# The delta rule's small steps placed by readiness, age and recent use of TensorE, between the dense blocks of a whole-model kernel

## Chip, cores, metric

The kernel runs on one core of a Trainium2 chip, in one launch. The metric is the device time of a run in microseconds; lower is better.

## What is computed

The input is 256 tokens of width 1024, in float32. Sixteen meta tokens are put before them (272 columns in the kernel). The first block has two layers, a gated DeltaNet and an mLSTM, each followed by a convolutional FFN; a second block of two layers has pooling, sparse attention and memory attention. The change matters in the gated DeltaNet. It is, cut to its core:

```
proj = h @ w_in                                   # dense: q, k, v, z, and the gates
kb = kc * bc[..., None]
a_mat = jnp.eye(CHUNK) + jnp.einsum('bhnid,bhnjd->bhnij', kb, kc) * decay * strict
sol = lax.linalg.triangular_solve(a_mat, rhs, left_side=True, lower=True)
attn = jnp.einsum('bhnid,bhnjd->bhnij', qc, kc) * decay
def step(S, xs):                                  # over the chunks, one after the other
    v_new = u_c - jnp.einsum('bhck,bhkv->bhcv', w_c, S)
    o_c = jnp.einsum('bhck,bhkv->bhcv', qd_c, S) + jnp.einsum('bhij,bhjv->bhiv', att_c, v_new)
    S = S * gt_c[..., None, None] + jnp.einsum('bhck,bhcv->bhkv', kt_c, v_new)
    return S, o_c
o = rms_norm(o, norm_w) * jax.nn.silu(z)
return o.reshape(B, L, GDN_VAL_DIM) @ w_out       # dense
```

The kernel takes chunks of 16, 128 and 128 tokens (c = 0, 1, 2) and inverts the triangular matrix itself, by doubling.

## The kernel before

**Dense work.** Weights stream from HBM through `ring` in slabs. Each half slab is split into a high part (`splitH`, by ScalarE) and a low part (`splitL`, by VectorE or GpSimd), and every dense product is three matmuls: aH with splitH, aH with splitL, aL with splitH. A dense block is these three for one slice of 128 of the contraction; in the DeltaNet stage they are 128x272. An output tile is eight blocks. The main program `gdn()` has four phases of eight tiles (`GDN_TILES`), one for each of four groups of heads (g = 0 to 3), and then 16 tiles for z. `gdn_out()` follows, the projection w_out, whose blocks read arenaR.

**Small steps.** Beside the main program run tasks, as generators, for group g and chunk c: `core(g)` makes keys, decays and products (its front), and then the recurrence over the chunks; `inv(g, 0)` and `tri(g, c)` invert the triangular matrices by levels of 16x16, 32x32 and 64x64 products; `vtr(g)` transposes v; `out(g, c)` normalizes and transposes the output. Each step is a handful of float32 matmuls that write one PSUM bank, and then work of VectorE, ScalarE or GpSimd before the task's next step can start. A float32 matmul that isn't a transpose has two records in the trace, so that `x4` in the order is `x8` there.

**The order.** `weave()` lays all into one list, `flow`, before the program is written, and each engine's instructions follow this list (`replay`). On the chip each engine runs its own in order and waits on semaphores. `weave()` runs a `Clock` for each engine, which holds planned costs; `settle()` moves them on. Each yield of a task gives the time at which it is due again: the end of the engines' planned work and 0.2 us. `one(due)` takes the task that has been due longest. It is called after each dense block until no task is due:

```
        if v != "go":
            while one(True):
                pass
```

A step is put off only where no PSUM bank of its pool is idle (`room`). Some steps hold the main program up: `until("vuse", 0, 2)` ahead of phase 3 (the recurrence of group 0 must have used its v), the z tiles wait for `until("out", gz, c)` of earlier groups, and `gdn_out()` waits at its ninth block for `until("out", 3, c)`, the last step of the last group. There is nothing dense to run at such a place.

## Time and profile before

| | |
|---|---|
| median of 3 runs | 1634.6 us (1634.51 to 1642.09) |
| the profiled execution, its own time | 1634.17 us |
| its span | 1632.4 us |
| PE busy | 1582.0 us of the span |
| mean granted TensorE clock | 0.952 of full speed |

The span is from the first to the last instruction; 1.8 us of the execution lie around it. PE is TensorE's matmul row. The granted clock is 1.00 at 2.4 GHz and 0.50 at 1.2 GHz; a mean between the two tells the share of time at each.

### The profile page before, as it was taken

The page shows a single profiled execution, that of the slowest core. Times are in us where ns is not written, and L with a number is a line of the kernel's source. Part 1 is how long each engine was busy: PE and PEld are TensorE (multiplying, and loading weights), DVE is VectorE, ACT ScalarE, POOL GpSimd, SP SyncE. Part 2 cuts the span into 40 slices and gives each one's busy share as a digit, 9 for nine tenths or more (in the row PEclk, how much of TensorE's full clock was granted, in tenths as well). Part 3 has the DMA queues.
Part 4 walks back from the last instruction along what each step waited for, and adds up shares of the span by engine and source line. Part 5 has one row for each costly group of instructions (what it writes and reads, how often), then busy time and mean ns, then how long its engine had stood idle before and what let it go on. Part 6 is the DMA issues. An engine that isn't in the chain of part 4 may idle for free.

```text
span 1632.4 us, 35024 instructions
## 1 busy us (share of the span) xinstructions
PE 1582.0 (97%) x14201; PEld 1488.6 (91%) x14201; DVE 1102.6 (68%) x2253; ACT 944.8 (58%) x1988; POOL 346.8 (21%) x412
## 2 busy tenths in 40 slices
PE   8998999999999999999999999999999989999998
PEld 6987987899899999987899999889999989899998
DVE  4776686558588864766689965667766666676663
ACT  6652664456376654546476754547676554667754
POOL 4231222133133322000423421003101210031010
PEclk9987797899799999999799999999999999999999
DMA  6320222035265554342346766545444645454452
GB/s 206 117 80 3 80 82 63 28 104 169 100 201 174 172 182 144 126 132 92 128 151 196 199 218 201 160 130 167 132 153 156 215 162 168 140 168 142 143 172 88
DMA packets 64976, 230.41 MB, mean 141 GB/s; under 512 B 7312, under 2 KB 9488, under 8 KB 64816
## 3 DMA queue, kind: packets, MB, share of 16 engines
q1 hardware_dynamic: 59792, 217.67, 42.3%
q0 software_dynamic: 4160, 8.98, 1.8%
q8 instruction: 113, 1.85, 0.5%
q10 hardware_dynamic: 864, 1.52, 0.3%
q14 instruction: 47, 0.39, 0.1%
HBM read 222.91 MB, written 5.24 MB: 140 GB/s over the span
## 4 chain that ended last, share of the span: by engine, by line
PE 77%; DVE 12%; ACT 5%; issue 3%; DMA 1%; POOL 1%; ACTq 0%; SPq 0%; DVEq 0%; POOLq 0%
PE ps L623 75%; DVE splitL L2305 4%; DVE arena L2313 3%; PE ps L627 3%; ACT splitH L1699 2%; ACT arena L1704 1%; DVE mixT L2310 1%; DVE arena L2310 1%; ACT L1704 1%; DVE arena L2321 1%; ACT sq L1704 1%; DMA ring<-wst 1%; POOL sq L3129 1%; ACT arenaR L1704 0%; DVE mixT L2313 0%
## 5 line engine op out<-in xcount | busy, mean ns | idle before, releaser
L2305 DVE TENSOR_TENSOR splitL<-ring,splitH 128x512 fp32r<-128x512 f32 x767 | 564.6, 765 | 244.0 <-ACT splitH L1699 235.5
L623 PE MATMUL ps<-aH,splitH 128*128 128x256 f32 (+2 forms) x2232 | 661.0, 297 | 13.4 <-DVE arena L2321 5.8
L623 PE MATMUL ps<-aH,splitL 128*128 128x256 f32 (+2 forms) x2232 | 640.5, 288 | 0.0
L623 PE MATMUL ps<-aL,splitH 128*128 128x256 f32 (+2 forms) x2232 | 626.8, 287 | 0.0
L1699 ACT ACTIVATE splitH<-ring 128x512 fp32r<-128x512 f32 x824 | 479.9, 622 | 130.5 <-PE ps L623 120.8
L623 PEld LDWEIGHTS ps<-aH,splitH 128*128 128x128 f32 x2232 | 429.8, 193 | 28.6 <-issue 11.5
L623 PEld LDWEIGHTS ps<-aH,splitL 128*128 128x128 f32 x2232 | 430.1, 193 | 0.0
L623 PEld LDWEIGHTS ps<-aL,splitH 128*128 128x128 f32 x2232 | 422.2, 192 | 0.4
L623 PE MATMUL ps<-arenaR,splitH 128*128 128x256 f32 (+2 forms) x1856 | 348.0, 288 | 3.0 <-POOL arenaR L3129 1.6
L623 PEld LDWEIGHTS ps<-arenaR,splitH 128*128 128x128 f32 x1856 | 290.9, 191 | 4.8 <-POOL arenaR L3129 1.9
L623 PE MATMUL ps<-arenaR,splitL 128*128 128x256 f32 (+2 forms) x928 | 264.2, 285 | 0.0
L1704 ACT ACTIVATE arena<-ps 128x256 f32<-128x256 f32 (+10 forms) x261 | 94.7, 367 | 185.5 <-PE ps L623 164.0
L623 PE MATMUL ps<-arena 32*32 32x32 f32 (+6 forms) x3144 | 177.6, 237 | 11.5 <-DVE arena L2310 9.6
L623 PEld LDWEIGHTS ps<-arenaR,splitL 128*128 128x128 f32 x928 | 176.7, 190 | 0.0
L623 PEld LDWEIGHTS ps<-arena 32*32 32x32 f32 (+4 forms) x3144 | 132.3, 137 | 45.8 <-issue 26.7
L2313 DVE SCALAR_TENSOR_TENSOR arena<-ps,vec_sb,arena 128x271 f32<-128x271 f32 (+4 forms) x275 | 135.2, 492 | 35.9 <-ACT arena L1704 30.4
L3129 POOL TENSOR_TENSOR arena<-arena 128x272 f32<-128x272 f32 (+4 forms) x79 | 73.2, 931 | 287.1 <-DVE arena L2313 145.2
L1704 ACT ACT_TABLE_LOAD x92 | 118.0, 1283 | 4.2 <-PEq L3589 1.7
L1704 ACT ACTIVATE arena<-ps,vec_sb 128x272 f32<-128x272 f32 (+5 forms) x154 | 74.2, 496 | 63.2 <-PE ps L623 61.7
L3124 POOL TENSOR_TENSOR splitL<-ring,splitH 128x512 fp32r<-128x512 f32 x57 | 77.4, 1367 | 141.5 <-ACT splitH L1699 140.7
L1704 ACT ACTIVATE arena<-arena 128x256 f32<-128x256 f32 (+10 forms) x137 | 64.2, 480 | 49.3 <-DVE arena L2313 26.8
L2321 DVE COPY arena<-ps 128x256 f32<-128x256 f32 (+9 forms) x138 | 51.8, 382 | 40.3 <-PE ps L623 34.6
(212 smaller groups left out, 1282.5 us busy)
## 6 DMA issues: line engine op xcount, KB each, us to landing
ring<-wst SPq DMA_DIRECT2D x412, 512.0 KB, 3.9
mem_scratch<-arenaR POOLq DMA_DIRECT2D x16, 128.0 KB, 4.3
arenaR<-mem_scratch POOLq DMA_DIRECT2D x4, 512.0 KB, 8.2
rel_scratch<-arena POOLq DMA_DIRECT2D x8, 255.5 KB, 3.6
arena<-x SPq DMA_DIRECT2D x2, 512.0 KB, 4.9
arena<-mem POOLq DMA_DIRECT2D x2, 512.0 KB, 4.3
arena<-rel_scratch POOLq DMA_DIRECT2D x1, 1024.0 KB, 9.1
out<-arena ACTq DMA_DIRECT2D x4, 256.0 KB, 2.1
```

The source lines that it names most:

```text
L623: return pe.matmul(out, lhsT, rhs, start=start, stop=stop)
L627: return pe.transpose(out, in_, ident[0:n, 0:n])
L1699: act.activation(hi, raw, ACT.Copy, bias=0.0, scale=1.0).then_inc(*inc(("hi", q)))
L1704: return act.activation(out, in_, f, bias=bias, scale=scale, accum_out=accum)
L2305: dve.tensor_tensor(lo, raw, hi.bitcast(F32), ALU.subtract).then_inc(*inc(("lo_dve", q)))
L2310: return dve.tensor_tensor(out, x, y, op)
L2313: return dve.scalar_tensor_tensor(out=out, in0=x, scalar=s, in1=y, op0=op0, op1=op1)
L2321: return dve.tensor_copy(out, x)
L3124: pool.tensor_tensor(lo, raw, hi.bitcast(F32), ALU.subtract).then_inc(*inc(("lo_pool", q)))
L3129: return pool.tensor_tensor(out, x, y, op)
```

## The change

`Array` is a Clock of its own for TensorE. It adds up the use of the array by each matmul, scaled by the rows that it fills, and doubles the planned cost of matmuls where the use before was low. It also holds a `credit`: use adds to it, planned time takes `RATE` of itself off it. `room` now names the semaphore events that a step waits for. A step is taken only when, by the planned clocks, its banks are free and its inputs are there, or else, while the main program is held up, when nothing else can go. Where before a due step was issued whether its inputs were there or not, it now gives the time at which they will be. Tasks of older groups are tried first (`rank`). And after a dense block the small steps go on only while the credit isn't negative. A bank is chosen by when it is free, and not in turn.

```
+def rank(name):
+
+    return name[1] - (name[0] == "out") if name[0] in ("core", "vtr", "inv", "tri", "out") else 0
...
+class Array(Clock):
...
+    RATE, MOST = 0.42, 1.5
...
+    def cost(self, x):
+        self.window()
+        us, use = x
+        self.use += use
+        us = us if self.full or us < 0.03 else 2 * us
+        self.credit = min(self.MOST, self.credit + use - self.RATE * (self.at + us - self.seen))
+        self.seen = self.at + us
+        return us
...
+    def side(limit):
+
+        late = []
+        for x in sorted(live, key=lambda x: (rank(x[0]), x[1])):
+            at = x[1]
+            if at <= pe.at:
+                at = advance(x, False)
+                if at is None:
+                    return True
+            if at < min(limit, NEVER):
+                late.append((at, x))
+        for at, x in sorted(late, key=lambda y: y[0]):
+            pe.at = max(pe.at, at)
+            if advance(x, True) is None:
+                return True
+        return False
...
+        follow(main)
         if v != "go":
-            while one(True):
+            while pe.credit >= 0 and side(0.0):
                 pass
...
-            def room(banks, n):
-                while dry and len(banks.idle) < n:
-                    yield WAIT
+            def room(banks, n, *events):
+
+                while dry:
+                    t = max([banks.ready(n)] + [pe.when.get(e, NEVER) for e in events]) + 0.1
+                    if t <= pe.at + 0.02 or pe.force and t < NEVER:
+                        break
+                    yield "at", t
...
-                    yield from room(bg, 1)
+                    yield from room(bg, 1, ("Tts", g, c, P // 2), ("rr", g, c) if c else ("vtok", g, 0))
                     b = bg.get("tr", g, c)
...
                     for m, (kind, x) in enumerate(tiles):
+                        yield from room(fg, 1)
                         for k in range(KD):
```

No instruction is added or removed: both programs have 12139 TensorE matmuls. The lines below 200 move by some, so that L623 of before is L690, L627 is L694, L2310 is L2378 and L2313 is L2381.

**TensorE, where the front of group 1 meets the inversion of group 0.** Before, from the end of a dense block on (aH with splitL). `cst_sb,sq` are the sums of squares of keys, 32x32 and 16x16 the levels of `tri` and `inv`, `cst_sb,arena` transposes of `core`. 36 steps stand there with no dense block among them, of which these are the first:

```order
L623 MATMUL ps<-aH,splitL 128x272
L623 MATMUL ps<-cst_sb,sq 16x1 x4
L623 MATMUL ps<-cst_sb,sq 128x1 x8
L623 MATMUL ps<-ssr,rst 16x16 x4
L623 MATMUL ps<-rst,ssr 16x16 x4
L623 MATMUL ps<-arena 32x32 x32
L627 MATMUL ps<-cst_sb,arena 16x128 x2
L627 MATMUL ps<-cst_sb,arena 128x128 x4
L623 MATMUL ps<-arena 32x32 x48
L623 MATMUL ps<-ssr 16x16 x4
L623 MATMUL ps<-arena 32x32 x16
L627 MATMUL ps<-cst_sb,arena 128x16
```

The changed kernel, at the same steps, from the transposes that follow the first level on:

```order
L694 MATMUL ps<-cst_sb,arena 16x128 x2
L690 MATMUL ps<-aH,splitH 128x272
L690 MATMUL ps<-aL,splitH 128x272
L690 MATMUL ps<-aH,splitL 128x272
L694 MATMUL ps<-cst_sb,arena 128x128 x2
L690 MATMUL ps<-aH,splitH 128x272
L690 MATMUL ps<-aL,splitH 128x272
L690 MATMUL ps<-aH,splitL 128x272
L690 MATMUL ps<-arena 32x32 x32
L690 MATMUL ps<-ssr 16x16 x4
L694 MATMUL ps<-cst_sb,arena 128x128 x2
L690 MATMUL ps<-aH,splitH 128x272
```

A dense block now stands after each step or two. The longest run at this place is 16 steps, a little later, and no longer 36. The matching place of groups 2 and 3 reads alike: 36 steps without a block before, 15 now.

**TensorE, the recurrence of group 3, the last one.** `sq,arena` is the product with the state S (two products of chunk 2), the 128x128 ones are the product with the inverse and, behind it, the one with the attention matrix; `cst_sb,mixT` is the transpose of the output. Before, one step of it with the dense blocks around it; 12 blocks follow before its next step:

```order
L623 MATMUL ps<-aH,splitL 128x272
L623 MATMUL ps<-sq,arena 128x256 x4
L623 MATMUL ps<-aH,splitH 128x272
L623 MATMUL ps<-aL,splitH 128x272
L623 MATMUL ps<-aH,splitL 128x272
L623 MATMUL ps<-aH,splitH 128x272
L623 MATMUL ps<-aL,splitH 128x272
L623 MATMUL ps<-aH,splitL 128x272
```

The changed kernel, from the last dense block ahead of the hold at `gdn_out()`'s ninth block to the first one behind it:

```order
L690 MATMUL ps<-arenaR,splitL 128x272
L690 MATMUL ps<-sq,arena 128x256 x4
L690 MATMUL ps<-arena 128x128 x4
L694 MATMUL ps<-cst_sb,mixT 128x16 x4
L690 MATMUL ps<-arena 128x256 x2
L690 MATMUL ps<-arena 128x128 x4
L690 MATMUL ps<-sq,arena 128x256 x4
L690 MATMUL ps<-arena 128x128 x4
L694 MATMUL ps<-cst_sb,mixT 128x128 x4
L690 MATMUL ps<-arena 128x128 x4
L694 MATMUL ps<-cst_sb,mixT 128x128 x4
L690 MATMUL ps<-arenaR,splitH 128x272 x2
```

Ten steps of group 3, its last two chunks, now stand in one run at the end with no dense block between them. Each but the transposes and the attention's products needs the one before it.

**VectorE, the same place.** `splitL<-ring,splitH` is the split of a half slab for the dense blocks, `arena<-ps,arena` x4 the right side of the recurrence, `mixT<-ps,arena` the product scaled. Before:

```order
L2313 SCALAR_TENSOR_TENSOR sq<-sq,arena,ps 128x128 x4
L2310 TENSOR_TENSOR mixT<-ps,mixT 128x512
L2305 TENSOR_TENSOR splitL<-ring,splitH 128x512
L2313 SCALAR_TENSOR_TENSOR arena<-ps,arena 128x128 x4
L2310 TENSOR_TENSOR mixT<-mixT,arena 128x4 x2
L2310 TENSOR_TENSOR arena<-arena 128x544
L2321 COPY arena<-ps 128x272
L2305 TENSOR_TENSOR splitL<-ring,splitH 128x512
L2310 TENSOR_TENSOR mixT<-ps,arena 128x512
L2658 RECIPROCAL mixT<-mixT 128x4
```

The changed kernel:

```order
L2381 SCALAR_TENSOR_TENSOR sq<-sq,arena,ps 128x128 x4
L2378 TENSOR_TENSOR mixT<-ps,mixT 128x512
L2381 SCALAR_TENSOR_TENSOR arena<-ps,arena 128x128 x4
L2378 TENSOR_TENSOR mixT<-mixT,arena 128x4 x2
L2378 TENSOR_TENSOR mixT<-ps,arena 128x512
L2726 RECIPROCAL mixT<-mixT 128x4
L2378 TENSOR_TENSOR mixT<-mixT,arena 128x4
L2378 TENSOR_TENSOR mixT<-mixT 128x512
L2378 TENSOR_TENSOR arena<-ps,arena 128x512
L2381 SCALAR_TENSOR_TENSOR arena<-ps,vec_sb,arena 128x4x128
L2378 TENSOR_TENSOR mixT<-ps,mixT 128x512
```

The splits have gone from between the recurrence's instructions, since no dense block is there that asks for them.

The five longest runs without a dense block held 36, 22, 36, 22 and 15 steps before; they hold 16, 15, 14, 13 and 10 steps now. Behind `gdn_out()`'s ninth block the two orders agree but for single steps that stand up to some two dozen blocks earlier or later.

## Rows read from the trace of the kernel before

**Rows 1.** The page: span, granted clock in 40 slices.

```profile
span 1632.4 us, 35024 instructions
...
PEclk9987797899799999999799999999999999999999
```

**Rows 2.** Windows of the stage: us, busy (records) per engine, granted clock, DMA.

```profile
97.70:370.50 272.80, 255.84 (x3904) 226.43 (x3904) 179.34 (x492) 135.95 (x350) 66.25 (x68) 0.83 0.19 60
...
97.70:123.70 26.00, 23.60 (x577) 19.67 (x576) 17.91 (x61) 12.09 (x34) 6.96 (x9) 0.70 0.14 44
123.70:171.60 47.90, 42.87 (x817) 35.27 (x816) 27.97 (x85) 14.60 (x53) 6.11 (x9) 0.71 0.01 3
...
205.40:224.50 19.10, 17.60 (x153) 15.94 (x152) 17.45 (x55) 10.49 (x30) 1.31 (x3) 1.00 0.19 60
250.00:313.50 63.50, 57.63 (x1352) 48.07 (x1353) 41.05 (x135) 25.10 (x84) 13.03 (x18) 0.73 0.09 28
313.50:370.50 57.00, 54.83 (x411) 52.21 (x410) 34.20 (x68) 34.09 (x73) 20.83 (x14) 0.94 0.32 102
```

**Rows 3.** Windows again, only PE instructions that touch splitL (one per dense block).

```profile
97.70:123.70 26.00, 0.08 (x1) 0.70 0.14 44
123.70:171.60 47.90, 4.58 (x12) 0.71 0.01 3
205.40:224.50 19.10, 1.52 (x6) 1.00 0.19 60
250.00:313.50 63.50, 2.21 (x7) 0.73 0.09 28
```

**Rows 4.** PE instruction groups in 97.7 to 370.5 us, by form.

```profile
L623 PE MATMUL ps<-aH,splitH 128*128 128x272 f32 x239 | 76.7, 321 | 0.0
L623 PE MATMUL ps<-aH,splitL 128*128 128x272 f32 x240 | 72.1, 300 | 0.0
L623 PE MATMUL ps<-aL,splitH 128*128 128x272 f32 x239 | 71.7, 300 | 0.0
L623 PE MATMUL ps<-arena 32*32 32x32 f32 x2176 | 36.0, 209 | 1.4 <-DVE arena L2615 0.8 <-DVE mixT L2310 0.5
...
L623 PE MATMUL ps<-sq,arena 128*128 128x256 f32 x64 | 18.6, 439 | 0.0
```

**Rows 5.** The chain in order of time, its long piece of dense work.

```profile
372.38 47.66 PE ps L623 x381
```

**Rows 6.** PE timeline at both clocks: start us, us, instruction.

```profile
82.71 0.45 PE L623 MATMUL ps<-arena 32*32 32x32 f32 x32
...
170.12 0.43 PE L623 MATMUL ps<-aH,splitH 128*128 128x272 f32 x1
170.35 0.43 PE L623 MATMUL ps<-aL,splitH 128*128 128x272 f32 x1
...
182.22 1.89 PE L623 MATMUL ps<-sq,arena 128*128 128x256 f32 x8
183.76 0.48 PE L623 MATMUL ps<-aH,splitH 128*128 128x272 f32 x1
```

**Rows 7.** PE timeline, steps of group 0's recurrence.

```profile
146.51 3.96 PE L623 MATMUL ps<-arena 128*128 128x256 f32 x76
...
150.96 1.99 PE L623 MATMUL ps<-sq,arena 128*128 128x256 f32 x8
...
159.70 0.55 PE L623 MATMUL ps<-arena 128*128 128x128 f32 x1 [3.03 <-DVE arena L2310]
```

**Rows 8.** DVE timeline, the same stretch and the last chunk of group 3.

```profile
148.62 1.12 DVE L2313 SCALAR_TENSOR_TENSOR sq<-sq,arena,ps 128x128 f32<-128x128 f32 x4 [1.67 <-PE ps L623]
...
152.13 1.13 DVE L2313 SCALAR_TENSOR_TENSOR arena<-ps,arena 128x128 f32<-128x128 f32 x4 [0.37 <-PE ps L623]
...
155.35 0.68 DVE L2310 TENSOR_TENSOR mixT<-ps,arena 128x512 f32<-128x512 f32 x1
...
356.25 0.69 DVE L2310 TENSOR_TENSOR mixT<-ps,mixT 128x512 f32<-128x512 f32 x1 [2.17 <-PE ps L623]
```

More of the change, by code:

```diff
@@ L152, in settle, with cost, transpose @@
         return len(self.open) < n
[L154 to L161 removed]
+    def cost(self, us):
+        return us
+    def transpose(self, out, in_):
+        return self.spend(0.1 + 1.04e-3 * size(in_))
     def activation(self, out, in_, f, bias=0.0, scale=1.0, accum_out=None):
@@ L187, with __init__, window, matmul @@
     tensor_tensor = tensor_scalar = scalar_tensor_tensor = tensor_copy = memset = tensor_tensor_scan = op
+class Array(Clock):
+    WINDOW, ENOUGH = 3.4133, 1.3
+    RATE, MOST = 0.42, 1.5
+    def __init__(self, when, phase=0.0):
+        super().__init__(0, 0, when)
+        self.end, self.use, self.full = phase, 0.0, False
+        self.credit, self.seen, self.force = 0.0, 0.0, False
+    def window(self):
+        while self.at >= self.end:
+            self.full, self.use, self.end = self.use >= self.ENOUGH, 0.0, self.end + self.WINDOW
+    def matmul(self, out, lhsT, rhs, start=True, stop=True):
+        n, m, k = size(rhs), size(lhsT), lhsT.shape[0]
+        if rhs.dtype == F32R:
+            return self.array(n * 0.4625e-3, k / 128, n / 2.4e3)
+        return self.array(0.027 if k == 32 == m == n else 2 * max(0.025, m / 1.2e3, 2 * n / 2.4e3), k / 128, 4 * n / 2.4e3)
+    def transpose(self, out, in_, ident):
+        n = in_.shape[0]
+        return self.array(max(0.025, n / 1.2e3), n / 128, 2 * n / 2.4e3)
+    def array(self, us, share, busy):
+        return self.spend((us, share * busy))
+    def cost(self, x):
[5 more added lines that the diff above has]
+        self.seen = self.at + us
+        return us
 def settle(clocks):
@@ L225, in __init__, with since, ready @@
         self.free = {}
+    def since(self, i):
+        return max([0.0] + [self.gate.eng.when.get(e, NEVER) for e in self.free.get(i, [])])
+    def ready(self, n):
+        return sorted(map(self.since, self.idle))[n - 1] if len(self.idle) >= n else NEVER
     def get(self, *key):
         if self.gate.dry:
-            i = self.idle.pop(0)
+            i = min(self.idle, key=self.since)
+            self.idle.remove(i)
             self.table[key] = i, self.free.get(i, [])
@@ L252, in weave, with made, follow @@
     pe = clocks[0]
-    def step(name):
-        made = [next(start_(name, g, p), None) for g, p in zip(gens, programs)]
-        settle(clocks)
-        return made[0]
-    def start_(name, g, p):
-        if name not in g:
-            g[name] = p[name[0]](*name[1:])
-        return g[name]
+    def made(name, n):
+        if name not in gens[n]:
+            gens[n][name] = programs[n][name[0]](*name[1:])
+        return gens[n][name]
+    def follow(name):
+        for n in range(1, len(programs)):
+            next(made(name, n), None)
+        used = [c for c in clocks[:4] if c.open]
+        settle(clocks)
+        flow.append(name)
+        return used
@@ L287, in weave @@
     start.append(spawn)
     main = ("main",)
-    for v in start_(main, gens[0], programs[0]):
-        if v == WAIT:
-            assert one(False), ("no task can go on", [x[0] for x in live])
+    for v in made(main, 0):
+        if isinstance(v, tuple):
+            if not side(v[1]):
+                assert v[1] < NEVER, ("no task can go on", [x[0] for x in live])
+                pe.at = max(pe.at, v[1])
             continue
-        for g, p in zip(gens[1:], programs[1:]):
-            next(start_(main, g, p), None)
-        settle(clocks)
-        flow.append(main)
+        follow(main)
@@ L898, in core @@
                 yield 1.8
-                yield from room(bg, 1)
+                yield from room(bg, 1, ("tsq", g))
                 b = bg.get("ss", g)
@@ L916, in core @@
                 for j in range(2):
-                    yield from room(bg, 1)
+                    yield from room(bg, 1, *(("ktok", g, c) for c in range(3)))
                     b = bg.get("kT2", g, j)
@@ L1147, in out @@
                 yield 0.1
-                yield from room(bg, 1)
+                yield from room(bg, 1, ("on", g, c))
                 b = bg.get("otr", g, c)
```

85 lines of the change are left out of this document (35 added, 50 removed).

## The prediction

> **What bounds the kernel now.** I read the page first. The span is 1632.4 us and the granted clock is high nearly everywhere but in slices 3 to 9, 11 and two single later slices [rows 1]. Those early slices are the gated DeltaNet, the one stage whose order the change alters much. The profiled execution took 1634.17 us, 1.8 us around its span; the median of the three runs is 1634.6 us, 0.4 us above it. The sum below is made against 1634.2, and half a per cent of it is 8.2 us.
>
> Then I took windows over the stage, from the last dense block ahead of the first bare run to the last small step of group 3: 97.7 to 370.5 us, 272.8 us, with a mean granted clock of 0.83 [rows 2]. With only two levels that is (1 - 0.83) x 2 x 272.8 = 93 us at 1.2 GHz. Neither VectorE (179.3 us busy) nor ScalarE (136.0 us) nor the DMAs (share 0.19) fill it [rows 2]. TensorE shows 255.8 us busy, but a matmul's record holds its way through the array, so records overlap and this is no measure of work. I price the work by distances between starts at the full clock:
> - Dense matmuls of 272 columns: a chain piece of 381 in 47.66 us gives 0.125 us each [rows 5]. There are 239 + 240 + 239 = 718 of them [rows 4]: 89.8 us.
> - 32x32 products: 32 in 0.45 us, 0.014 us each [rows 6], 2176 of them [rows 4]: 30.6 us.
> - The 128x256 products with the state: 8 in 183.76 - 182.22 = 1.54 us, 0.193 each [rows 6], 64 of them [rows 4]: 12.3 us.
> - What is left of the 3904 records is 946 of many forms, from 16x16 to 128x256. I take 0.076 us for each, an estimate between the 0.014 and the 0.193 above, nearer to the 0.096 that half of 256 columns would take: 71.9 us.
>
> Together 204.6 us. So 272.8 - 204.6 = **68 us of the stage are excess**: waits for the other engines, and a slow array.
>
> Where is it? Three windows are almost bare of dense blocks: 97.7 to 123.7, 123.7 to 171.6 and 250.0 to 313.5, 137.4 us in all, with 2746 records [rows 2] but only 1 + 12 + 7 = 20 blocks [rows 3]. Their clock is 0.70, 0.71 and 0.73 [rows 2], which makes 78 of the 93 us at 1.2 GHz. Sixty dense matmuls are 7.5 us. The rest of the stage holds 135.4 us, 658 dense matmuls (82.3 us) and about 500 small records, 38 us at 0.076: an excess of 15 us. That leaves 114.8 - 38 = 77 us of small work to the bare windows, and to them 137.4 - 7.5 - 77 = **53 us of the excess**. Per microsecond of small work that is 0.69.
>
> **Not every bare run costs this.** The window 205.4 to 224.5 holds the front of group 2, with transposes and products of 128 columns, and 6 blocks [rows 3]. Its clock stayed at 1.00 [rows 2]. Of 153 records 18 at most are dense (2.3 us); 135 small ones at 0.10, since nearly all are 128 wide, are 13.5 us; 3.3 us of 19.1 are excess, 0.25 per microsecond of small work. The runs that lose much are those of 32x32, 16x16 and 64x64 levels, where each step waits for the one before and the array does little.
>
> A rule of the Trainium skill speaks against counting on this window. TensorE: Matmul & The Clock Gate, in its part 4 on the PE-mode transpose, says that transposes don't count as activity for the clock as matmuls do, while the changed planner counts them as use and gives credit for them. By the rule such fronts would fall to the low clock. The trace doesn't bear it out where it can be seen, since the window above kept its 1.00, though half of its small work is no transpose.
>
> **What the change does to it.** Nothing is added or removed, so the 204.6 us stay. Only the order differs, and with it the engines' waits. VectorE and ScalarE follow the same list; VectorE has 272.8 - 179.3 = 93 us free in the stage, so a stage 25 us shorter still has room. No DMA is moved past another: SP issues the slabs in the same order, and at a share of 0.19 a slab is early. GpSimd's small steps move with their tasks; it is busy 66.3 of 272.8 us.
>
> From the order I counted runs without a dense block and priced them as above. Before, the same 250 blocks are parted by steps at 40 places, now at 81, for about 210 steps. The runs of the changed kernel that hold over 1.5 us of small work:
> - Two fronts of 9.5 and 9.3 us (groups 2 and 3). At 0.25 they cost **5 us**. Before, one of them stood in a window that cost 3.3 and the other in a bare one.
> - Two runs of levels and recurrence, 7.6 us (16 steps) and 7.4 us (13 steps, the hold ahead of phase 3), and some eight shorter ones of 2.0 to 4.7 us, 25 in sum: 40 us. At 0.69 they would cost 28 us, at nothing 0. With dense blocks close on both sides the array has less time to fall, and each wait is shared with fewer steps. I take a third, 0.33: **13 us**. The choice is mine, and the widest one here.
> - The last run, 8.4 us of small work in ten steps that wait for each other. Before, they stood among dense blocks and their waits were covered. Priced as a chain: product with S to the end of vn 156.03 - 150.96 = 5.1 us [rows 7, 8] and 0.7 for vs behind it; state product to the end of S 149.74 - 146.51 = 3.2 [rows 7, 8]; the next chunk 5.1 again; the attention product to the end of its sum 0.69 + 2.17 = 2.9 [rows 8], since VectorE waited 2.17 us for it; and 5 us for the norm and the last transpose, an estimate from four squares, a root and three small VectorE steps of the sizes in these rows. That is 22 us for 8.4 of work: **13.5 us** of cost. It could be 8 if steps of the two chunks overlap, 18 if the clock is low throughout.
> - Everything else, in reach of dense blocks: 15 us before. I keep **15 us**. Some of it is dense work that still ran at 1.2 GHz behind a bare run, 0.23 us a matmul (170.12 to 170.35 [rows 6]) and not 0.125; that part should shrink, while single waits like the 3.03 us ahead of 159.70 [rows 7] may now fall between blocks.
>
> Sum: 5 + 13 + 13.5 + 15 = 46.5 us of excess for 68. The stage becomes 21.5 us shorter, 1634.2 - 21.5 = 1612.7; I say **1612 us**. Behind the DeltaNet the order changes by single steps inside dense stretches, which wait for nothing that TensorE needs; I price it at zero, with 2 us either way.
>
> **The rivals.**
> - *The low clock all but goes.* The levels' runs cost nothing and the covered part drops to 8 us: 5 + 0 + 13.5 + 8 = 26.5, 41.5 us less, 1593 us. For it: 78 of the 93 us at 1.2 GHz stood in bare windows. Against it: steps of one chain still wait for each other at the hold ahead of phase 3. Chance 0.16.
> - *The holds eat the gain.* The levels' runs cost their old 0.69 (28 us) and the last run 18: 5 + 28 + 18 + 15 = 66, 1632 us, the same. For it: blocks that are spread thinly among 32x32 levels may leave the clock low and then run at 0.23 themselves. A band around this case, 1626 to 1642, has chance 0.22.
> - *Just in time is too late (slower).* Steps are now put a tenth of a microsecond behind the planned end of their inputs. If the real end is later, TensorE stands with dense blocks behind the step that can't pass it. Idle was 272.8 - 255.8 = 17 us for some 210 steps before, 0.08 each [rows 2]. At 0.2 us more for each, 42 us, the time is 1612 + 42 = 1654. It decides from (21.5 + 8.2) / 210 = 0.14 us a step. Against it: before, too, a step was taken 0.2 us after planned ends, without heed of its inputs. Chance 0.12.
> - *The forecast's case*, 10 to 35 us less: chance 0.50.
>
> **How the numbers follow.** The range goes from the first rival, 1594, to the second, 1634, which leaves out the slower case and the edges. The likeliest case alone is 1600 to 1624. Faster by over 8.2 us: 0.50 + 0.16 + the lower edge of the second rival, 0.05: 0.71. The same: 0.17. Slower: 0.12.
>
> **What would show it.** The stage's windows in the changed profile: about 251 us where 272.8 stood, with a granted clock near 0.90 (some 50 us at 1.2 GHz). Windows around the front of group 1 with a clock above 0.8. One new stretch of about 22 us ahead of `gdn_out()`'s ninth block with no dense matmul, and in it waits of TensorE for VectorE and ScalarE. The page's slices behind the stage as before. I am wrong in the size of the third term if that last stretch takes 30 us, in the second if the clock stays under 0.8 between the blocks, and in the mechanism if the clock rises and TensorE's idle time grows by as much.

## The result and the profile after

The changed kernel takes 1625.36 us (median of 10 runs, 1619.16 to 1632.66), the kernel before 1635.86 us (10 runs, 1630.93 to 1642.18). The ratio is 0.9938, with an interval of [0.9914, 0.9963]: faster by 0.6%, some 10 us, where 22 us were forecast. The profiled execution took 1628.06 us for a span of 1626.3. TensorE's lines 623 and 627 are now 690 and 694; VectorE's 2310 and 2313 are 2378 and 2381.

The page of the changed kernel, its span and the granted clock in 40 slices, against [rows 1]:

```profile
span 1626.3 us, 35018 instructions
...
PEclk9998699989799999999799999999999999999999
```

Before, slices 3, 4, 5, 7 and 8 stood at 7 or 8. Now 4 and 9 stand at 8 and slice 5 at 6; the rest of the stage is at 9, and slice 11 is as it was. The higher clock is there, and much of the time is not. The windows of the changed kernel say where it is (us, busy and records of PE, PEld, DVE, ACT and POOL, clock, DMA share, GB/s), against [rows 2]:

```profile
47.20:421.50 374.30, 360.23 (x4919) 326.35 (x4917) 253.79 (x640) 202.08 (x484) 104.42 (x105) 0.90 0.27 84
96.00:120.00 24.00, 22.47 (x573) 19.28 (x573) 16.60 (x56) 12.58 (x34) 6.02 (x9) 0.95 0.15 47
96.00:366.10 270.10, 256.59 (x3940) 225.50 (x3939) 184.21 (x500) 139.03 (x354) 69.71 (x69) 0.89 0.21 66
148.90:161.50 12.60, 10.50 (x197) 8.97 (x196) 8.85 (x25) 7.57 (x19) 0.41 (x2) 0.86 0.15 48
166.30:200.90 34.60, 34.60 (x478) 29.27 (x477) 19.89 (x61) 15.74 (x48) 6.16 (x8) 0.63 0.07 17
205.00:300.00 95.00, 94.96 (x1636) 84.80 (x1636) 70.26 (x192) 51.79 (x133) 29.56 (x29) 0.98 0.26 80
343.20:366.10 22.90, 13.70 (x67) 11.12 (x65) 14.85 (x39) 6.83 (x23) 0.00 (x0) 0.79 0.07 23
```

The stage is the third row, the front of group 1 the second. The window holds a few records more than the 3904 of [rows 2], 9 of them dense matmuls; priced as in the prediction that is 3.2 us of work more. So its excess is 270.1 - 204.6 - 3.2 = 62 us, for 68 before. I forecast 46.5. Yet the clock is 0.89 and 95 us in the middle run at 0.98, where [rows 2] had 63.5 us at 0.73. From 205 to 300 TensorE is also never idle (94.96 of 95.00 us), though its work there is spread one or two steps at a time. The low clock that is left is bunched: 34.6 us behind the hold ahead of phase 3 ran at 0.63 (fifth row). That is (1 - 0.63) x 2 x 34.6 = 26 us at 1.2 GHz, of 59 in the stage by the same sum.

Stretches that hold the same work in both kernels compare better. I gave every record to its step of the written order and counted by dense blocks from the program's start. Blocks 60 to 566, with everything between them, are this row of the kernel before:

```profile
45.60:429.00 383.40, 364.49 (x4931) 331.38 (x4929) 256.74 (x652) 201.34 (x483) 101.12 (x106) 0.87 0.26 82
```

The changed kernel's is the first row of the table above: 374.3 us, 9.1 us less. The same count gives 365.0 and 361.9 us for blocks 1130 to 1900, and 565.6 and 569.6 us for blocks 1900 to 3200. The forecast's stage is blocks 161 to 447, inside the first stretch.

### The profile page after: what moved, and what is told of

It is laid out like the page before. It is cut to its first block, busy times and chain, and to the rows that moved or that the text cites. A ratio compares the mean times of both kernels' runs of the same rounds, so it can differ in the third digit from the quotient of the medians.

```text
span 1626.3 us, 35018 instructions
## 1 busy us (share of the span) xinstructions
PE 1581.7 (97%) x14201; PEld 1486.6 (91%) x14201; DVE 1104.0 (68%) x2253; ACT 947.2 (58%) x1990; POOL 348.0 (21%) x412
## 4 chain that ended last, share of the span: by engine, by line
PE 83%; DVE 7%; ACT 4%; issue 4%; POOL 2%; DMA 1%; SPq 0%; ACTq 0%; POOLq 0%
PE ps L690 80%; PE ps L694 3%; DVE splitL L2373 3%; DVE arena L2381 2%; ACT splitH L1767 1%; POOL sq L3197 1%; ACT arena L1772 1%; DVE mixT L2378 1%; DMA ring<-wst 1%; ACT arenaR L1772 1%; DVE mixT L2381 0%; ACT L1772 0%; DVE arena L2378 0%; DVE arena L2385 0%; ACT sq L1772 0%
## 5 line engine op out<-in xcount | busy, mean ns | idle before, releaser
L690 PE MATMUL ps<-aH,splitH 128*128 128x256 f32 (+2 forms) x2232 | 665.4, 299 | 7.2 <-ACT aH L1772 5.4
L690 PE MATMUL ps<-aH,splitL 128*128 128x256 f32 (+2 forms) x2232 | 641.3, 288 | 0.0
L690 PE MATMUL ps<-aL,splitH 128*128 128x256 f32 (+2 forms) x2232 | 627.1, 287 | 0.0
L690 PEld LDWEIGHTS ps<-aH,splitH 128*128 128x128 f32 x2232 | 430.4, 193 | 23.3 <-issue 12.3
L690 PEld LDWEIGHTS ps<-aH,splitL 128*128 128x128 f32 x2232 | 430.8, 193 | 0.0
L690 PEld LDWEIGHTS ps<-aL,splitH 128*128 128x128 f32 x2232 | 422.4, 192 | 0.5
L690 PE MATMUL ps<-arenaR,splitH 128*128 128x256 f32 (+2 forms) x1856 | 350.9, 289 | 3.1 <-POOL arenaR L3197 2.0
L690 PEld LDWEIGHTS ps<-arenaR,splitH 128*128 128x128 f32 x1856 | 293.0, 192 | 6.0 <-POOL arenaR L3197 1.9
L690 PE MATMUL ps<-arenaR,splitL 128*128 128x256 f32 (+2 forms) x928 | 265.2, 286 | 0.0
L690 PEld LDWEIGHTS ps<-arenaR,splitL 128*128 128x128 f32 x928 | 178.0, 192 | 0.0
L1772 ACT ACTIVATE arena<-ps 128x256 f32<-128x256 f32 (+9 forms) x261 | 94.2, 366 | 143.4 <-PE ps L690 116.0
L690 PE MATMUL ps<-arena 32*32 32x32 f32 (+7 forms) x3144 | 168.6, 226 | 7.8 <-DVE arena L2381 3.4
L690 PEld LDWEIGHTS ps<-arena 32*32 32x32 f32 (+5 forms) x3144 | 123.9, 128 | 44.2 <-issue 26.5
L2381 DVE SCALAR_TENSOR_TENSOR arena<-ps,vec_sb,arena 128x271 f32<-128x271 f32 (+4 forms) x275 | 135.4, 493 | 36.5 <-ACT arena L1772 29.2
L1772 ACT ACTIVATE arena<-ps,vec_sb 128x272 f32<-128x272 f32 (+6 forms) x154 | 74.3, 497 | 78.4 <-PE ps L690 68.5
L3197 POOL TENSOR_TENSOR sq<-sq,arena 128x256 f32<-128x256 f32 x32 | 27.0, 843 | 200.5 <-DVE arena L2378 200.5
```

The costliest lines, as they stand in the source:

```text
L690: return pe.matmul(out, lhsT, rhs, start=start, stop=stop)
L1772: return act.activation(out, in_, f, bias=bias, scale=scale, accum_out=accum)
L2381: return dve.scalar_tensor_tensor(out=out, in0=x, scalar=s, in1=y, op0=op0, op1=op1)
L3197: return pool.tensor_tensor(out, x, y, op)
```

## The experiments

All kernels below are the changed one with the edit shown, but e9 (the kernel before with an edit). Ratios are to the kernel before, run on the same chip in turn; its median there was 1633.2 to 1637.0 us. e13 to e16 ran on another chip than e1 to e12, so runs are compared by their ratios, each with its interval. "Part" is the time of blocks 60 to 566 in the one profiled execution, and a place is one at which small steps part the dense blocks of the stage: 40 before, 82 in the changed kernel.

**e1, no credit**: the rule that spreads blocks by the array's use is gone.

```
-            while pe.credit >= 0 and side(0.0):
+            while side(0.0):
```

> One part undone: after a dense block small steps go on whatever the credit is. The order agrees with the changed kernel's up to about block 220 of the DeltaNet, and later has other runs: the last bare run holds 5 steps (4.1 us of small work) where the changed kernel has 10 (8.4 us, 22.9 us long); the places where small steps part the dense blocks stay 82. Theory A (the credit keeps the clock up, and is what the gain came from): the granted clock of the stage falls back towards 0.83 and the time to that of the kernel before, 1635. Theory B (the gain came from taking steps when their inputs are there; the credit costs a late bare run): the clock stays within 0.02 of 0.89 and the time is 3 to 8 us below the changed kernel, 1617 to 1622.

1617.43 us, 0.9891 [0.9872, 0.9911], part 368.1 us. Theory B is borne out: the credit is no source of the gain. Its interval ends at 0.9911 and the changed kernel's begins at 0.9914, so that it was even a small loss is shown, but barely. The plan tells what the credit does. Some blocks ahead of the last hold TensorE's planned clock takes a wait, the credit falls below zero and is still at -0.35 at the hold, and the steps of group 3 are held back until then. Without it the last run has five steps and not ten; the timeline of e1 there (start, us, instruction, wait) is short:

```profile
345.36 2.44 PE L690 MATMUL ps<-sq,arena 128*128 128x256 f32 x8 [2.86 <-DVE sq L2381]
350.16 2.08 PE L690 MATMUL ps<-arena 128*128 128x128 f32 x8 [2.36 <-DVE arena L2381]
353.02 2.08 PE L690 MATMUL ps<-arena 128*128 128x128 f32 x8 [0.78 <-DVE arena L2378]
354.89 1.06 PE L694 MATMUL ps<-cst_sb,mixT 128*128 128x128 f32 x4
359.05 1.12 PE L694 MATMUL ps<-cst_sb,mixT 128*128 128x128 f32 x4 [3.10 <-DVE mixT L2378]
359.82 0.80 PE L690 MATMUL ps<-arenaR,splitH 128*128 128x272 f32 x2
```

It ends at 359.8, 17.3 us with the wait ahead of it, where the changed kernel's ends at 366.1 and takes 22.9.

**e2, no rank**: `rank()` returns 0, so older groups don't go ahead. **e3, no readiness**: a step needs a free bank only, not its inputs. **e4, a larger margin**: inputs must be there 0.5 us, not 0.1 us, ahead.

```
e2: -    return name[1] - (name[0] == "out") if name[0] in (...) else 0
    +    return 0
e3: -                    t = max([banks.ready(n)] + [pe.when.get(e, NEVER) for e in events]) + 0.1
    +                    t = pe.at if len(banks.idle) >= n else NEVER
e4: -... for e in events]) + 0.1
    +... for e in events]) + 0.5
```

> One part undone: older groups are no longer ahead. The order then has two long bare runs, 34 steps (18.2 us of small work) ahead of phase 3 and 28 steps (14.9 us) at the first z tile, since the recurrence that the main program waits for is late; 76 places. Theory A (long bare runs cost 0.69 us per us of small work, as in the kernel before): 26 us more small work in long runs than in the changed kernel at those places gives 12 to 18 us more, 1637 to 1643. Theory B (the age rule does nothing that readiness and credit don't): 1623 to 1628.

> One part undone: a due step is taken without heed of whether its inputs are there, as before; age and credit stay. 55 places and not 82, no bare run at the end, but one of 32 steps (16.1 us of small work). Theory A (readiness is the gain): TensorE waits for inputs, idle time in the stage doubles from 13.5 us, the time is 1635 or more. Theory B (each passage from small steps back to dense work costs the 0.19 us that the two traces show in both kernels, so that 27 fewer save 5 us, and the missing last run saves 14, against 8 to 10 for the long run): 1613 to 1620.

> One number changed: a step is taken 0.5 us behind the planned end of its inputs and not 0.1. 72 places, the last run holds 9 steps (6.9 us). Theory A (steps are placed just too early, the planned ends are early by some tenths, and TensorE stands): idle time in the stage falls under 8 us and the time by 4 us or more, to 1620 or less. Theory B (lateness isn't what ate the gain): within 3 us of the changed kernel, 1622 to 1628.

Theory B each time. e2: 1625.3 us, 0.9934 [0.9912, 0.9956]: as the changed kernel. e3: 1617.57 us, 0.9898 [0.9876, 0.992], part 363.8 us with 55 places: the readiness rule isn't the gain either. e4: 1622.73 us, 0.9927 [0.9905, 0.9949], within theory B's range. So none of these rules alone is needed for what was gained. But e4's stage did change: its part took 364.0 us at a clock of 0.94, 10.3 us less than the changed kernel's, while TensorE's idle time in it rose from 13.6 to 18.7 us. It wasn't fewer late inputs, then; the clock was higher and the last run took 18.1 us for 22.9. Some 4 us went back in blocks 1130 to 1900, most of it as idle time. e2's part took 369.6 us: its two long runs, 27.0 and 23.2 us in the trace, had a clock of 0.81 and 0.78, and still the part took no longer than the changed order in e13 (below).

**e5 and e6, what a passage costs.** One (e5) or four (e6) 32x32 float32 products stand ahead of each of 363 dense tiles of the whole program, 321 of them between two dense blocks that followed each other. They write into a bank that the tile then overwrites.

```
+                    for _ in range(0 if dry else 1):      # e6: 4
+                        mm(psum[b][0:32, 0:32], ident[0:32, 0:32], ident[0:32, 0:32])
                     for k in range(K):
```

> The disputed cost by itself. The changed kernel, with one 32x32 float32 product more ahead of the first block of each of 363 dense tiles, in the tile's own PSUM bank, which the block then clears: the result is the same, and at 321 places a dense matmul stands right ahead, so that 321 passages are new. Theory A (a passage from dense to small and back costs the 0.19 us that the traces show, whatever is between, and the product itself some 0.03): 321 x 0.19 + 363 x 0.03 = 72 us more, about 1697. Theory B (0.19 us was the time of the small steps' own matmuls, of their weights or of a wait for their inputs): 363 x 0.03 = 11 us more, about 1636.

> The same with four such products in a row in place of one: no passage more than with one. Theory A: the three others cost 3 x 363 x 0.03 = 33 us over the kernel with one, about 1730, which shows what one product costs without a passage. Theory B: also 33 us over the kernel with one, but from 1636 to 1669. If four cost four times what one costs, it is the products and not the passages.

Theory A, and dearer than it had it. e5: 1735.35 us, 1.0619 [1.0563, 1.0674], 110 us over the changed kernel. e6: 1799.84 us, 1.1013 [1.0956, 1.1071], 64.5 us over e5, with two runs of each. Three products more cost 64.5 / 363 = 0.18 us, 0.059 each, and the first one costs 110 / 363 = 0.30. So a passage from dense to small and back costs (110 - 363 x 0.059) / 321 = **0.28 us**, where the small work is 32x32 products. e5's timeline shows one:

```profile
900.35 0.28 PE L690 MATMUL ps<-aH,splitL 128*128 128x258 f32 x1
900.56 0.24 PE L690 MATMUL ps<-cst_sb 32*32 32x32 f32 x2
900.74 0.39 PE L690 MATMUL ps<-aH,splitH 128*128 128x258 f32 x1
900.96 0.28 PE L690 MATMUL ps<-aL,splitH 128*128 128x258 f32 x1
901.08 0.28 PE L690 MATMUL ps<-aH,splitL 128*128 128x258 f32 x1
```

Starts are 0.12 us apart within dense work. Here the small product starts 0.21 behind the last dense one, and the second dense matmul 0.22 behind the first: its 0.39 us are those of a matmul that stood. The engine shows no idle time in it.

**e7, age only** (e1's and e3's edits), and **e8, prices only** (e1's, e2's and e3's). **e9** goes from the other side: the kernel before, with the new `Array` prices alone.

> Two parts undone at once: a due step is taken whether its inputs are there or not, and whatever the credit is. Left are the age rule and the planned prices (a doubled price where the array was little used). 59 places; one run of 38 steps (19.3 us of small work) at the front of group 3, no bare run at the end. Theory A (readiness and credit each cost as much as they gave, the gain is in the age rule and the prices): 1615 to 1621, as without one of them. Theory B (one of the two is needed, either will do): 1628 or more.

> All three rules undone (readiness, credit, age); only the planned prices, the choice of banks and the wait for a free bank ahead of a tile stay. 59 places, the longest runs hold 20 steps (13.3 us), 17 (11.6) and 17 (8.2). Theory A (the prices, which put dense blocks and small steps in better proportion, are the gain): within 4 us of the kernel with age alone. Theory B (age is the gain): the time of the kernel before, 1632 or more.

> One part done alone: the kernel before with nothing but the changed kernel's planned prices (a matmul costs twice as much in the plan where the array was little used before it). Due times, age and room are as before. 54 places in place of 40; the two bare runs of 36 steps (15.7 us of small work each) become one of 29 (18.6 us) and several of 3 to 9 us; no bare run at the end. Theory A (the prices are the gain, the three rules give nothing on top): 1618 to 1625, at or under the changed kernel. Theory B (the rules are needed): 1630 or more.

e7, between its two theories: 1625.96 us, 0.9957 [0.9937, 0.9978]; without either rule the gains of e1 and e3 are gone again. e8, within 4 us of it as theory A had it: 1622.24 us, 0.9916 [0.9886, 0.9947]. e9: 1649.61 us, 1.0089 [1.0064, 1.0114], slower than before. Parts 373.5, 376.6 and 385.0 us. One new wait of 4.1 us for ScalarE in the attention part is in e9, whose blocks 1900 to 3200 take 572.7 us for 565.6. I had taken e8 and e9 for nearly the same order; 27 us between them say that the order isn't a sum of its rules.

**e10, the rules with flat prices**: a matmul is no longer planned at double length when the array was little used. The doubling spares only what is planned under 0.03 us, such as the 32x32 products; dense matmuls it doubles too.

```
-        us = us if self.full or us < 0.03 else 2 * us
+        us = us
```

> The other part alone: readiness, age and credit as in the changed kernel, but a matmul's planned price no longer doubles. 63 places, runs of 33 steps (17.3 us of small work), 25 (11.3), 18 (12.0) and a last bare run of 7 (5.8 us). Theory A (prices are the gain): the long runs and the last one cost what they did before, 1632 or more. Theory B (the rules gain by themselves): 1622 to 1628.

1614.7 us, 0.9875 [0.9851, 0.99]. Neither theory had it: A is wrong, and B's 1622 to 1628 is too slow. I had not expected a gain of 10.7 us over the changed kernel. The part takes 371.0 us, just 3.3 less than in the changed kernel.

**e11, the passage priced** at 0.12 us each way in the plan with e4's margin, and **e12**, the same price with e7's edits.

```
+        us += 0.12 * (dense != self.dense)
+        self.dense = dense
```

> The changed kernel with two numbers mended by what the runs showed: each passage between dense and small work costs 0.12 us in the plan, and a step is taken 0.5 us behind its inputs' planned end. 85 places, the longest runs 9.6 and 7.7 us of small work, and no bare run at the end, since group 3 is done at block 394. Theory A (a plan that knows the passage keeps its clocks nearer to the chip's, and the missing last run saves about 14 us, against nothing more for 3 places): 1610 to 1616. Theory B (the number of passages decides, and 85 are as dear as 82): 1620 to 1626.

> The kernel with age alone (no readiness, no credit), with the passage priced at 0.12 us in the plan. 65 places, the longest runs are two fronts of 10.7 and 8.9 us and one of 7.0 (12 steps); group 3 is done by block 345. Theory A (few passages and no long run of levels): 65 places cost 3 us less than 82, no last run saves 14: 1608 to 1616, the best of all. Theory B (without readiness TensorE waits for late inputs): 1620 or more, with idle time in the stage over 18 us.

Neither gave what theory A had. e11: 1629.97 us, 0.997 [0.9947, 0.9993], slower than theory B too, with 85 places. Its part is short, 367.5 us at a clock of 0.93; blocks 1130 to 1900 take some 7 us more. e12: 1648.71 us, 1.0096 [1.0063, 1.0128], its part 394.0 us. Theory B has it: idle time in the stage was 20.1 us, and the clock of the part fell to 0.86. A price alone tells the plan how long a passage lasts; no rule in it chooses fewer of them.

**e13 to e16, the program in two halves.** A flag turns at the start of the mLSTM's task `mlv`, behind the DeltaNet. e13 has the changed kernel's order ahead of it and, word for word, the order of before behind it. e14 doubles prices ahead of it only, e15 behind it only. e16 is e14 with e3's edit.

```
+        pe.flat = True if ("mlv",) in names else pe.flat
-        us = us if self.full or us < 0.03 else 2 * us
+        us = us if self.full or us < 0.03 or self.flat else 2 * us
e13, and: -            while pe.credit >= 0 and side(0.0):
          +            while (pe.flat or pe.credit >= 0) and side(0.0):
          +  with pe.flat, room() asks for a free bank only and get() takes the first
```

> Work order of the changed kernel up to the end of the DeltaNet stage (to the point where the mLSTM's task mlv is started), and from there on the order of the kernel before, instruction for instruction. Theory A (the gain of 10 us is all made in the DeltaNet part, and the changes in the rest cancel): 1624 to 1628 us, by the traces' 383.4 against 374.3 us for blocks 60 to 566 and 930.6 against 931.5 us for blocks 1130 to 3200. Theory B (the rest of the changed kernel has a real loss, hidden by a gain in the same rest that depends on the new rules): the same time, but the 3.5 us wait of TensorE for VectorE's mixT near 1162.8 us is gone while the 2 to 3 us of blocks 1130 to 1900 are given back. Under 1620: the rest of the changed kernel is a loss as a whole.

> The changed kernel, with the planner's doubled price for small products in force up to the end of the DeltaNet part only: the order of the changed kernel there, and that of the kernel with flat prices (e10) behind it. Theory A (most of the 11 us that flat prices gave lie in the attention part, where the doubled price moves the heads' steps): 1614 to 1618 us. Theory B (they lie in the DeltaNet part): 1621 to 1626 us.

> The other half: flat prices up to the end of the DeltaNet part, doubled ones behind it. Theory A (the loss is in the attention part): 1620 to 1624 us, 3 us under the changed kernel by the traces' 371.0 against 374.3 us for blocks 60 to 566. Theory B (it is in the DeltaNet part): 1613 to 1617 us. Together with e14 the two halves should add up to e10's 10.7 us, within 3 us, if the halves don't act on one another.

> The changed kernel without the readiness rule, with the doubled price in the DeltaNet part only: the DeltaNet order of e3 (363.8 us for blocks 60 to 566, against 374.3), and flat prices behind it. Theory A (the two gains, fewer passages with no hold in front of the last run, and flat prices in the attention part, add up): 1603 to 1609 us, the fastest of all. Theory B (without readiness the attention part picks badly whatever its prices): 1612 to 1618 us.

e13: 1622.69 us, 0.9925 [0.9896, 0.9955]. e14: 1617.82 us, 0.9885 [0.9858, 0.9912]. e15: 1620.39 us, 0.9908 [0.9885, 0.9931]. e16: 1612.32 us, 0.9856 [0.9831, 0.9881], the lowest median, at the near edge of theory B. The gains of e3 and e14 over the changed kernel would add up to 0.9845, which its interval holds, so whether they add up in full isn't shown, nor is it told from e10. e13, a little under theory A's 1624, gives the changed DeltaNet order 0.75%, 12 us, all of the gain; the changed rest added nothing that can be told from zero. Its trace has the signs of theory B, though: the wait near 1162.8 us is gone and blocks 1130 to 1900 take 3.4 us more, so that the changed rest holds a loss and a gain of like size (below). e14, as theory A had it, says that flat prices behind the DeltaNet are worth 0.5%, 9 us (0.9938 against 0.9885); its interval ends at 0.9912, just short of the changed kernel's 0.9914, and e10's, with the same order there, lies clear of it. e15 lies in theory A's reach too, but overlaps the changed kernel, so the other half's share is open. Together the two halves make 12.5 us, for e10's 10.7.

e13 and e14 have the changed kernel's order up to block 566, so their windows are two more executions of the same instructions. e13, then e14:

```profile
47.10:417.00 369.90, 355.78 (x4919) 322.08 (x4917) 253.37 (x639) 201.45 (x484) 103.45 (x105) 0.92 0.27 85
```

```profile
47.10:415.60 368.50, 354.07 (x4920) 320.54 (x4918) 252.73 (x641) 201.43 (x484) 103.52 (x105) 0.93 0.28 85
```

They took 4.4 and 5.8 us less than the changed kernel's own profile, at a clock of 0.92 and 0.93 for 0.90. So the changed kernel's own profile overstates what is left to explain, by about 5 us over the part. The three gains are 9.1, 13.5 and 14.9 us, 12.5 in the mean, and that agrees with e13's 12.

## Why the prediction was right and wrong

**The direction and the range held, the size didn't**: 10 us for 22. The rest of the program was priced at nothing, and its sum was nothing that e13 can tell, but not for the reason given. What fell short is the stage: blocks 161 to 447 took 278.9 us before and 271.4, 269.1 and 269.2 us in the three executions of the changed order, 7.5 to 9.8 us less where 21.5 were forecast. The part gained some 2 to 5 us more outside of them.

**Term 1, the two fronts: right.** 4.8 us for 5. With their work priced as before, one cost 3.5 and one 1.3 us. The front of group 1 kept a clock of 0.95 in the window from 96 to 120. The rule of the Trainium skill that I weighed (TensorE: Matmul & The Clock Gate, part 4, transposes are no activity for the clock) is not tested by it: 16 of the window's 573 records are transposes. Nor was it tested by the forecast's window from 205.4 to 224.5, where 28 of 153 are, far fewer than the half that I wrote.

**Term 2, runs of levels and recurrence: right in sum.** By the same sum over runs it is about 13 us: 2.3 for the run from 105.6 to 115.5, 5.2 for the hold ahead of phase 3 (the 12.6 us window at 0.86), the rest in short ones. A third of the old price was a choice that happened to fit. It fits this execution; in e13's the blocks around the hold took 19.8 us for 16.9.

**Term 3, the last run: right, in its place and its length.** I wrote 22 us for ten steps. The timeline of the changed kernel has 22.9, from 343.24 to 366.09:

```profile
343.24 1.89 PE L690 MATMUL ps<-sq,arena 128*128 128x256 f32 x8
348.22 1.13 PE L690 MATMUL ps<-arena 128*128 128x128 f32 x8 [3.09 <-DVE arena L2381]
349.71 0.61 PE L694 MATMUL ps<-cst_sb,mixT 16*128 16x16 f32 x4 [0.36 <-DVE mixT L2378]
351.03 3.78 PE L690 MATMUL ps<-arena 128*128 128x256 f32 x12 [0.72 <-DVE arena L2378]
354.61 2.77 PE L690 MATMUL ps<-sq,arena 128*128 128x256 f32 x8
357.74 1.16 PE L690 MATMUL ps<-arena 128*128 128x128 f32 x8 [0.35 <-DVE arena L2381]
359.61 0.66 PE L694 MATMUL ps<-cst_sb,mixT 128*128 128x128 f32 x4 [0.72 <-DVE mixT L2378]
360.22 1.16 PE L690 MATMUL ps<-arena 128*128 128x128 f32 x8
365.33 1.11 PE L694 MATMUL ps<-cst_sb,mixT 128*128 128x128 f32 x4 [3.95 <-DVE mixT L2378]
366.09 0.80 PE L690 MATMUL ps<-arenaR,splitH 128*128 128x272 f32 x2
366.69 0.43 PE L690 MATMUL ps<-arenaR,splitL 128*128 128x272 f32 x1
366.92 0.43 PE L690 MATMUL ps<-arenaR,splitH 128*128 128x272 f32 x1
```

Product with S, wait for VectorE, state product, product with S again, and a last wait of 3.95 us for the norm: the chain that the forecast put together from [rows 7, 8]. It leaves the clock low behind it (0.23 us from 366.69 to 366.92, at 1.2 GHz), and the dense blocks that follow start slow. Less 8.4 us of work it cost 14.5, for 13.5.

**Term 4 failed: "Everything else, in reach of dense blocks: 15 us before. I keep 15 us."** What is left of the 62 us is 62 - 4.8 - 13 - 14.5 = 30 us, about 28 in e13's and e14's executions. (The 15 even held the 3.3 us of a front that term 1 prices again.) Two things stand in it. The prediction counted the first, "parted by steps at 40 places, now at 81" (82 by the trace), and gave it no price. A stretch of the changed kernel's timeline at the full clock:

```profile
265.10 0.96 PE L690 MATMUL ps<-arena 64*64 64x64 f32 x16
265.99 0.39 PE L690 MATMUL ps<-aH,splitH 128*128 128x272 f32 x1
266.22 0.29 PE L690 MATMUL ps<-aL,splitH 128*128 128x272 f32 x1
266.34 0.28 PE L690 MATMUL ps<-aH,splitL 128*128 128x272 f32 x1
266.46 1.05 PE L690 MATMUL ps<-arena 128*128 128x128 f32 x8
267.45 0.36 PE L690 MATMUL ps<-cst_sb,arena 16*16 16x16 f32 x8
267.74 0.39 PE L690 MATMUL ps<-aH,splitH 128*128 128x272 f32 x1
```

One block of three matmuls, priced at 3 x 0.125 = 0.38 us, fills the time from 265.99 to 266.46, 0.47, with 0.23 between its first two starts; some more is lost ahead of the first. In blocks 161 to 447 a dense run at the full clock takes a median of 0.19 us over its price, alike for runs of one block and of many, in both kernels. It isn't alike for all small work: over six traces (before, changed, e1, e4, e13, e14) it is 0.20 between 32x32 products (55 runs) and 0.09 between 128x128 ones (12 runs), as here where 128x128 products follow the block. The 42 places more are 42 x 0.19 = 8 us, or 12 at the 0.28 of e5 and e6. All dense runs of these blocks together took 17.7 us over their price before and 25.0 in the changed kernel, 25.1 and 25.3 in e13 and e14. Split by the clock, the same blocks give the account of the change:

| excess of blocks 161 to 447, us | before | changed |
|---|---|---|
| runs that touch 1.2 GHz | 62.8 | 44.5 |
| runs at the full clock throughout | 12.3 | 23.1 |
| both | 75.1 | 67.6 |

Runs at the low clock lost 18.3 us less, close to what was forecast for the whole; runs at the full clock lost 10.8 more, which the 8 to 12 us of the passages would fill. (The sum before is above 68 because this count prices each kind of step by its own fastest occurrence.) That a passage costs 0.28 us at 32x32 products is shown by e5 and e6. That passages took this share here is worked out from the trace and not shown by an experiment. e3 speaks for it (55 places, part 10.5 us shorter at a better clock), but its order differs in more than the places, and over all runs the places don't decide:

| run | places | part, us | clock of the part |
|---|---|---|---|
| e4 | 72 | 364.0 | 0.94 |
| e11 | 85 | 367.5 | 0.93 |
| e1 | 82 | 368.1 | 0.93 |
| e3, and e16 with its order | 55 | 363.8, 366.6 | 0.92 |
| e2 | 76 | 369.6 | 0.92 |
| e10, and e15 with its order | 63 | 371.0, 372.1 | 0.92 |
| e7 | 59 | 373.5 | 0.92 |
| e8 | 59 | 376.6 | 0.91 |
| e9 | 54 | 385.0 | 0.91 |
| changed, e13, e14 | 82 | 374.3, 369.9, 368.5 | 0.90, 0.92, 0.93 |
| before | 40 | 383.4 | 0.87 |
| e12 | 65 | 394.0 | 0.86 |

The time goes with the clock more than with the places. e4, with 72 places, took 19.4 us off the kernel before in its one profile, nearly the forecast; so passages alone don't explain why the changed kernel didn't.

The second thing in term 4 is dense and small work that still ran at 1.2 GHz; I wrote that this part "should shrink". The same blocks behind the hold ahead of phase 3, in the changed kernel and then in e13:

```profile
165.30:201.20 35.90, 35.90 (x495) 30.37 (x491) 20.66 (x63) 16.17 (x50) 6.16 (x8) 0.64 0.07 18
```

```profile
164.20:193.70 29.50, 29.50 (x496) 24.99 (x492) 17.59 (x57) 14.34 (x49) 4.88 (x7) 0.83 0.06 19
```

They were never idle, and the same instructions took 6.4 us longer at the lower clock. How much of term 4 is this and how much passages differs by execution and is open.

**The rivals.** *The low clock all but goes* was half right, on the clock, and wrong in time for this order; e4 comes nearest to it. *The holds eat the gain* (1632 us): the last run cost 14.5, not 18, and the levels' runs 13, not 28; "blocks spread thinly" did lose, by passages at the full clock and, behind the hold, by running at 1.2 GHz as this rival had it. *Just in time is too late* fell: TensorE's idle time in the stage went from 17 to 13.5 us (270.10 - 256.59), where 42 more were that rival's price, and e4's larger margin didn't lower the idle time. My test of the mechanism, a clock that rises with idle time that grows as much, could not have caught what happened, since neither a passage nor a low clock shows as idle time. The Trainium skill says as much in Perfetto Trace Analysis, Identifying the Most-Contended Engine: that the matmul busy share is not a good measure of how close TensorE is to its roofline; the window from 205 to 300 us, 94.96 of 95.00 us busy with the passages in it, agrees.

**Behind the DeltaNet** the orders are not all alike, and TensorE does wait there, which I did not see. The waits of TensorE from 1100 to 1500 us (us in total, times, longest), in the kernel before, the changed kernel and e14:

```profile
PE ps L623 <- DVE arena L2321: 3.3, 1, 3.3
PE ps L623 <- POOL mixT L3129: 1.1, 1, 1.1
```

```profile
PE ps L690 <- DVE mixT L2381: 4.5, 2, 3.5
PE ps L690 <- POOL mixT L3197: 1.4, 1, 1.4
```

```profile
PE ps L692 <- POOL mixT L3199: 2.1, 1, 2.1
```

The wait for VectorE of 3.3 us, or 3.5, is gone in e14, with flat prices. In the changed kernel it begins at 1162.8 us, and behind it matmuls of 256 columns start 0.21 us apart, at 1.2 GHz, till about 1172:

```profile
1166.33 1.22 PE L690 MATMUL ps<-sq,splitH 128*128 128x256 f32 x2 [3.50 <-DVE mixT L2381]
...
1170.12 0.41 PE L690 MATMUL ps<-aL,splitH 128*128 128x256 f32 x1
1170.33 0.41 PE L690 MATMUL ps<-aH,splitL 128*128 128x256 f32 x1
...
1172.35 0.28 PE L690 MATMUL ps<-aH,splitH 128*128 128x256 f32 x1
1172.46 0.28 PE L690 MATMUL ps<-aL,splitH 128*128 128x256 f32 x1
```

Blocks 2120 to 2320, which hold it, take 99.2 us in the changed kernel, 92.7 in e15 and 92.4 before and in e13, which place the small steps otherwise there; e15 has its wait of 3.5 us later, near 1458 us. So one such wait with its slow stretch costs some 6.5 us. Against it the changed kernel saves 3.1 us in blocks 1130 to 1900, and 5.1 in the 80 blocks around the 3.3 us wait of the kernel before, which take 36.9 us for 42.0. That the rest came out at zero is such a balance, and luck. e14 has neither wait, and its blocks 1130 to 3200 take 10.5 us less in the profile than the changed kernel's. Why the plan's doubled price puts a step into that place, and what e10's flat prices do in the DeltaNet, are open. e14 puts the whole at 0.5%. e16, the lowest median, does without the readiness rule, and without the doubled price behind the DeltaNet.

## What to carry to other kernels

Before steps are spread among dense work to keep the clock up, count how many times the array will go over from one kind to the other, and price each: here 0.28 us at 32x32 products, most of a block of 0.38. But don't count alone: the orders here with the fewest places were not the fastest, since their clock was lower. Spreading in portions of several steps, or only where the trace shows a low clock, is the idea that follows; no run here tests it.

A busy share near 1 and a granted clock near 1 don't mean that the engine does its work at its pace: compare the distances between starts with those of an undisturbed stretch.

When a planner's rules are changed together, take them out one at a time and then by stage. Here credit, rank and readiness could each go alone without loss, credit and readiness taken out together gained nothing, and the doubled price was a loss in one half. And look at the stage as well as the total: e4's total hid 10 us won in one stage.

## What the runs showed of the hardware

- A passage from dense matmuls (128x256 to 128x272) to one 32x32 float32 product and back costs 0.28 us by e5 and e6. On the dense side alone the traces have a median of 0.19 us: 0.20 between 32x32 products, 0.09 between 128x128 ones. Part of it hides in the first dense record, 0.39 us long for 0.28. What causes it no run tells.
- A 32x32 float32 product (two records) in a short sequence costs 0.059 us (e6 against e5), twice the 0.028 that two records take in a row of 32 [rows 6].
- The same instructions in the same order, blocks 60 to 566, took 374.3, 369.9 and 368.5 us in three executions, with a granted clock of 0.90, 0.92 and 0.93. An effect under 5 us in one stage isn't to be read from one pair of profiles.
- One wait of 3.5 us in dense work was followed by several us at 1.2 GHz, so that it cost about twice its length.
